# Expert additions as a TensorE loop, a ring of eight row buffers instead of ten, and query products every nine gathers

## The reference, cut to what matters

```python
def peer_mixer(h, w_q, keys_1, keys_2, u_tab, v_tab):
    q = (hf @ w_q).reshape(t, PEER_HEADS, PEER_QUERY_DIM)           # 8 heads, 256 wide
    s1 = jnp.einsum('thd,nd->thn', q[..., :half], keys_1)           # 128 keys
    s2 = jnp.einsum('thd,nd->thn', q[..., half:], keys_2)
    v1, i1 = lax.top_k(s1, PEER_TOPK)                               # 16 of each
    v2, i2 = lax.top_k(s2, PEER_TOPK)
    sc, ci = lax.top_k(cand, PEER_TOPK)                             # 16 of 256 sums
    experts = (e1 * PEER_N_KEYS + e2)
    gates = jax.nn.softmax(sc, axis=-1)
    def expert_block(args):                                         # 128 tokens at a time
        a = jax.nn.gelu(jnp.einsum('td,ted->te', hb, u_tab[eb]))
        w = gb * a
        return jnp.einsum('te,ted->td', w, v_tab[eb])
```

## Time and profile before

| | |
|---|---|
| median of 3 runs | 1461.5 us (1459.98 to 1465.24) |
| the profiled execution | 1459.02 us, span of the trace 1457.4 us |
| PE busy | 1295.8 us (89%) |
| DVE busy | 936.4 us (64%) |
| ACT busy | 658.5 us (45%) |
| POOL busy | 396.4 us (27%) |
| first gather issued, last gather issued | 164.3 us, 798.1 us |
| last gather landed | 819.4 us |

### The profile page before, as it was taken

The page is one execution under the profiler, slowest core; times in us unless marked ns, Lnnn a source line. Parts: engine busy times, 40 slices in busy tenths (PEclk is TensorE's granted clock), DMA queues, the critical chain, the costliest instruction groups (busy, mean ns, idle before and its releaser), DMA issues.

```text
span 1457.4 us, 21059 instructions
## 1 busy us (share of the span) xinstructions
PE 1295.8 (89%) x6856; PEld 930.2 (64%) x6856; DVE 936.4 (64%) x2259; ACT 658.5 (45%) x1809; POOL 396.4 (27%) x440
## 2 busy tenths in 40 slices
PE   6999888988888888777787888999999999999998
PEld 3888744434433343222332467899998887899897
DVE  6678787766767666766664566655556744655555
ACT  3444344443443434333433336555545448545554
POOL 4112345544444444444443142200001004100000
PEclk9999999999999999999999998999999999999999
DMA  8877799999999999999999621765556530455554
GB/s 330 339 265 282 272 420 420 421 423 420 421 422 421 420 421 421 422 421 422 421 421 422 246 74 43 255 203 181 184 187 240 193 116 2 159 161 186 186 187 145
DMA packets 81340, 422.50 MB, mean 290 GB/s; under 512 B 10144, under 2 KB 11472, under 8 KB 48368
## 3 DMA queue, kind: packets, MB, share of 16 engines
q0 software_dynamic: 47808, 307.91, 51.6%
q1 hardware_dynamic: 32128, 110.48, 22.7%
q10 hardware_dynamic: 1328, 3.15, 0.6%
HBM read 418.88 MB, written 2.62 MB: 289 GB/s over the span
## 4 chain that ended last, share of the span: by engine, by line
PE 54%; DMA 26%; DVE 11%; ACT 4%; issue 2%; POOL 1%; DVEq 0%; ACTq 0%; SPq 0%; POOLq 0%
DMA big<-in_experts,R 25%; PE pacc L1174 9%; PE pu L705 6%; PE pu L707 6%; PE pu L706 6%; PE pu L678 3%; DVE big L2477 3%; PE pacc L705 2%; PE pacc L706 2%; PE pacc L707 2%; PE pacc L763 2%; PE pacc L762 2%; PE pacc L764 2%; PE pu L688 1%; PE pu L1093 1%
## 5 line engine op out<-in xcount | busy, mean ns | idle before, releaser
L1174 PE MATMUL pacc<-big,early_l 128*128 128x512 f32 x1024 | 481.1, 612 | 106.8 <-ACT early_l L1508 106.8
L1174 PEld LDWEIGHTS pacc<-big,early_l 128*128 128x128 f32 x1024 | 187.3, 193 | 382.7 <-issue 380.2
L2477 DVE CUSTOM_DVE_ANT_0 big<-big,early_h 128x1024 f32<-128x1024 f32 x256 | 310.7, 1225 | 185.9 <-DMA big<-in_experts,R 184.7
L581 POOL DMA_INDIRECT big<-in_experts,R x256 | 289.5, 1131 | 363.6 <-PE pacc L1174 329.4
L463 DVE TENSOR_TENSOR ring_lo<-ring,ring_hi 128x512 fp32r<-128x512 f32 x336 | 220.0, 696 | 193.8 <-ACT ring_hi L456 193.6
L456 ACT ACTIVATE ring_hi<-ring 128x512 fp32r<-128x512 f32 x336 | 192.4, 620 | 135.2 <-PE pu L707 53.1
L1508 ACT ACTIVATE R<-R 128x1 f32<-128x1 f32 x256 | 51.4, 201 | 296.5 <-DVE R L2477 296.3
L705 PE MATMUL pu<-X2h,ring_hi 128*128 128x256 f32 x512 | 146.3, 286 | 3.2 <-DVE big L2592 3.2
L707 PE MATMUL pu<-X2h,ring_lo 128*128 128x256 f32 x512 | 145.5, 284 | 0.0
L706 PE MATMUL pu<-X2l,ring_hi 128*128 128x256 f32 x512 | 145.4, 284 | 0.0
L705 PEld LDWEIGHTS pu<-X2h,ring_hi 128*128 128x128 f32 x512 | 98.8, 193 | 4.3 <-DVE big L2592 3.6
(11 more groups left out here) (433 smaller groups left out, 2101.1 us busy)
## 6 DMA issues: line engine op xcount, KB each, us to landing
ring<-in_weights SPq DMA_DIRECT2D x208, 512.0 KB, 3.5
big<-in_ada POOLq DMA_DIRECT2D x40, 512.0 KB, 6.4
big<-in_w POOLq DMA_DIRECT2D x12, 512.0 KB, 7.4
big<-in_experts,R POOLq DMA_INDIRECT x256, 19.3
big<-in_late_q POOLq DMA_DIRECT2D x6, 512.0 KB, 8.9
bias_row<-big ACTq DMA_DIRECT2D x1, 1536.0 KB, 19.9
XT<-in_xT ACTq DMA_DIRECT2D x1, 1024.0 KB, 8.2
scr<-in_ada POOLq DMA_DIRECT2D x2, 512.0 KB, 12.2
```

Of the source, the lines that this page charges most:

```text
L581: pool.indirect_dma_start(out=pair_rows[:, m % PAIR_SLOTS, :], out_offset=None, in_=experts_d, in_offset=bass.IndirectOffsetOnAxis(ap=expe ...
L1174: last = mm(paccf[:, tt * D + half * 512:tt * D + (half + 1) * 512], diagonal[:, m % 16, :], pair_rows[:, m % PAIR_SLOTS, D + half * 512:D ...
L2477: v.tensor_tensor_reduce(out=pair_rows[:, m % PAIR_SLOTS, 0:D], in0=pair_rows[:, m % PAIR_SLOTS, 0:D], in1=h2_rows[:, u % TT, :], scale=1. ...
```

## The change

Four things change. The ring of row buffers has eight entries. Queries 4 to 15 come every nine gathers, at m = 9, 18, ... 108. Row additions 112 to 239 run as a loop of four rounds with a body of 32 additions (two units); in it the waits for the landing and for the diagonal count with the round's register. The accumulation of the first token tile's sums is closed by four small products with zeros after the loop, instead of by the `stop` flag of row addition 239, so ACT waits for one row addition more before it reads them. POOL's wait for `ada_used` at m = 8 goes, since from m = 8 on a gather waits for a row addition.

```diff
-PAIR_SLOTS = 10
+PAIR_SLOTS = 8
-QUERY_STEP = 12
+QUERY_STEP = 9
+LOOP_FIRST, LOOP_STEP = 112, 2 * TOPK
...
                 if m >= PAIR_SLOTS:
                     pool.wait_ge(s["rows_added"], m - PAIR_SLOTS + 1)
-                elif m in (4, 5, 8):
-                    pool.wait_ge(s["ada_used"], MOD_EARLY + {4: 5, 5: 7, 8: 8}[m])
+                elif m in (4, 5):
+                    pool.wait_ge(s["ada_used"], MOD_EARLY + {4: 5, 5: 7}[m])
...
-            pe.wait_ge(s["peer_copied"], EARLY_QUERIES + 2)
-            for m in range(PAIRS):
-                if query_at(m) is not None:
-                    query(query_at(m))
-                pe.wait_ge(*pair_landed(m))
-                pe.wait_ge(s["diagonals"], m + 1)
+            def add_rows(m, g=None):
+
+                sem, landed = pair_landed(m)
+                pe.wait_ge(sem, tick(g, 16 * LOOP_STEP // PAIR_SLOTS, landed))
+                pe.wait_ge(s["diagonals"], tick(g, LOOP_STEP, m + 1))
                 tt = m // TOPK % TT
                 for half in range(2):
                     last = mm(paccf[:, tt * D + half * 512:tt * D + (half + 1) * 512], diagonal[:, m % 16, :],
                               pair_rows[:, m % PAIR_SLOTS, D + half * 512:D + (half + 1) * 512],
-                              start=(m in (0, TOPK)), stop=(m in (PAIRS - TOPK - 1, PAIRS - 1)), skip_group_check=True)
+                              start=(m in (0, TOPK)), stop=(m == PAIRS - 1), skip_group_check=True)
                 last.then_inc(s["rows_added"], 1)
+
+            pe.wait_ge(s["peer_copied"], EARLY_QUERIES + 2)
+            for m in range(LOOP_FIRST):
+                if query_at(m) is not None:
+                    query(query_at(m))
+                add_rows(m)
                 if m >= 2 and query_at(m - 2) is not None:
                     key_scores(query_at(m - 2))
+            with pe.Fori(0, (PAIRS - TOPK - LOOP_FIRST) // LOOP_STEP) as g:
+                for m in range(LOOP_FIRST, LOOP_FIRST + LOOP_STEP):
+                    add_rows(m, g)
+            for b in range(4):
+                mm(paccf[:, b * T:(b + 1) * T], zeros[:, 0:P], zeros[:, :], start=False, stop=True, skip_group_check=True)
+            for m in range(PAIRS - TOPK, PAIRS):
+                add_rows(m)
                 if m == TURN:
                     turn_back(0)
             turn_back(1)
...
                 if m == TURN - 2:
-                    act.wait_ge(s["rows_added"], PAIRS - TOPK)
+                    act.wait_ge(s["rows_added"], PAIRS - TOPK + 1)
```

## The result

The changed kernel takes 1466.99 us (median of 8 runs, 1465.47 to 1467.94), the kernel before 1461.15 us beside it (8 runs, 1459.21 to 1465.24). The ratio of their times is 1.0037, with a 95% interval of 1.0028 to 1.0047. That is 5.4 us more, between 4.1 and 6.9 (the two medians alone are 5.8 us apart). 1465 was forecast, 3.2 us more than before, with a range of 1459 to 1475.

What follows compares the result with a forecast made beforehand. The prediction took the PEER layer to be bound by 256 gathers passing the DMA engines. It added 2.7 (ring at the start) + 0.3 + 0.2 (closer queries) = 3.2 us to 1461.5, giving 1464.7, stated as 1465, range 1459 to 1475.

Steps and rivals of the forecast that it cites:

- What bounds the kernel: PEER layer: 256 gathers at 2.49 us each through the DMA engines; time in which these run dry is lost one for one.
- The ring at the start: Eight buffers let the DMA engines run dry before gathers 11 to 13: +2.7 us; a slip of 1 to 7 us had chance 0.56.
- L: Time from issue to landing of an unqueued gather: taken as 5.4 us, bounded by 2.49 and 7.7 us.
- The ring in the steady part: Later gathers with eight buffers: 14.7 us from issue to landing leaves 7 to 9 us of room, cost 0.
- Closer queries: Queries every nine gathers: query 4 delays gather 17 by 0.3 us, query 5 adds 0.2, then 0 up to m = 108.
- rival 1: PE becomes the bound between gathers 20 and 110: 10 us lost, about 1472 us, slower; chance 0.22.
- The loop: Row additions 112 to 239 in rounds of 32: branches and register waits hidden under the DMA queue, cost 0.
- The prediction's own sign of being wrong: DMA engines also dry after 230 us, or at a turn of the loop, or dry nowhere.
- 2, no slip: At the start the queue never runs dry, or the first gathers return sooner: no change, 1461.5 us; chance 0.15.
- 3, code fetch at a turn: Turning back the loop fetches code at ten us a turn, three turns cost 3 to 9 us: about 1471 us; chance 0.03.
- 4, faster behind the gathers: Something in the later layers, such as PE's clock, comes out faster: below 1454 us; chance 0.04.
- the sum for L = 7.7 us: With an unqueued gather at 7.7 us: 5.0 + 0.3 + 0.2 = 5.5 us later at the last landing.

Runs made afterwards that it cites:

- six open: Kernel before, ten buffers, with POOL allowed only six unfinished gathers from gather 64 on: 1464.18 us, ratio 1.0024.
- late queries: Changed kernel with queries 4 to 15 at m = 20, 31, ... 141 and its loop from 144: 1466.47 us, ratio 1.0042 to the kernel before.
- the ring alone: Kernel before with eight row buffers in place of ten, queries still every twelve gathers, all row additions unrolled: 1465.70 us, ratio 1.0026.
- the kernel with three open: Kernel before, ten buffers, with POOL allowed only three unfinished gathers from gather 160 on: 1575.47 us in one run.
- Eight late: Kernel before, ten buffers, with at most eight unfinished gathers from gather 64 on: 1461.11 us, ratio 1.0001.
- the kernel with the later gates: Changed kernel with unit 1's exponential on ACT at m = 7 in place of 3, DVE's part at 10 in place of 5: 1465.16 us, ratio 1.0035.
- the last one: Changed kernel with unit 1's gates later, query 3 at m = 6, unit 2's searches later, queries 4 to 15 at 20, 31, ... 141: 1463.84 us, ratio 1.0023.
- Two pairs of kernels: Eight buffers and queries every nine, unrolled 1.0041, with loop 1.0037; eight buffers and queries every twelve, unrolled 1.0026, with loop 1.0028.

## Why the prediction was right, and where it was not

**What bounds the kernel: right.** In the changed kernel, dry time of the DMA engines came out in the landings nearly one for one (6.2 to 6.6 us of it against 6.5). As a rule "lost one for one" is too strong: the kernels with six open and with late queries lack about 10 and 8 us of bytes by 798 us, and have +5.6 and +4.4 us at the landings. Why is open.

**The ring at the start, 2.7 us (3.0 with query 4): right in mechanism and place, too small.** In the changed kernel 3.6 us are lost there, with the ring alone 4.1, and 3.8 [2.2, 5.3] in time. Counted from the first landing, gathers 11 to 14 landed 1.2, 1.8, 3.1 and 4.2 us later than before, where 0.3, 1.6, 2.7 and 2.4 were forecast. The term that was off is L, taken as one number. I took 5.4 us, and these four took 6.4, 5.6, 5.8 and 7.7 us from issue to landing. The last of them, issued 1.7 us behind gather 13, sets the slip, and it was costed at 2.4. The 5.4 was also luckier than its source: the transfer of the earlier trace rows did not run by itself, since 0.34 MB of weights moved beside it between 1266 and 1269 us. The other thing the forecast left out is that gathers before number 11 aren't free either: the stretch from 190 to 200 us, ahead of most of them, already lacks 1.1 us.

The Trainium skill's figure (DMA: Bandwidth & Descriptors, Anatomy of one DMA) made L an estimated 4.4 us, which the prediction set beside its own. The trace of the kernel with three open disagrees with it for these gathers: none landed in under 5.4 us.

**The ring in the steady part, 0: right in time.** Eight late cost 0.01% [-0.08, 0.10]; the one trace has 1.5 us.

**Closer queries, 0.3 + 0.2, then 0 up to m = 108: the step that failed.** The 0 was measured at 2.6 to 3.0 us. I put the chance of more at rival 1 and reckoned with averages, 21.0 us of PE work in 22.4. That average holds; PE is busy 161.25 of 182 us, where 165 was reckoned. What happens is two stalls. The step of nine puts some query work on the gathers with m % 16 = 13, where ACT takes the exponentials of the gates: the key scores of the query at 27 come at m = 29, and query 8 stands at m = 45. ACT in the changed kernel, in order of time, and then PE from 262 to 322 us:

```profile
261.55 0.38 ACT L1521 ACTIVATE big<-pm 128x256 f32<-128x256 f32 x1 [3.80 <-PE pm L1123]
261.95 1.28 ACT L1521 ACT_TABLE_LOAD   x1
...
263.67 1.28 ACT L1521 ACT_TABLE_LOAD   x1
```

```profile
265.89 12.12 PE L1174 MATMUL pacc<-big,early_l 128*128 128x512 f32 x24 [4.38 <-ACT early_l L1521]
...
302.12 1.88 PE L1174 MATMUL pacc<-big,early_l 128*128 128x512 f32 x4
306.72 5.32 PE L1174 MATMUL pacc<-big,early_l 128*128 128x512 f32 x8 [2.72 <-ACT early_l L1521]
```

ACT waits for the key scores, copies them, and then needs two table loads of 1.28 us around the exponential before it can make the next diagonal (`early_l` in the rows). PE waits 4.38 us for it. At gather 45 ACT waits for the product of the query instead, and PE waits 2.72 us. Then comes a second cost. The granted clock is 0.83 in the windows 260 to 270 and 300 to 310, which means that PE's clock stood at 1.2 in place of 2.4 GHz for 3.4 us of each, from the end of these waits on. The six additions from 265.89 take 12.12 us, where six at 1.74 take 10.4. The backlog reaches POOL some buffers later, and the DMA engines run dry from 270 and from 310 us on. The clock fell at about 266 us in all four traces that have the step of nine.

That the coincidence on ACT makes the waits is shown by the runs that move the queries. With queries at m = 20, 31, ... 141 the coincidences lie at gather 77 (scores) and 141 (query), and in both kernels with that schedule PE waits 4.38 us at the first and 2.72 at the second. All six kernels that have the coincidences have exactly these two waits; in those with the old step no PE wait between 190 and 560 us is over 2.5 us. Moving the exponentials away from those gathers was not tried.

How the cost splits between the wait and the clock is less certain. Behind the wait of 4.38 us the clock fell in all six. Behind that of 2.72 us it fell in four. The kernel with the later gates is one of the two where it did not:

```profile
300.00:310.00 10.00, 7.28 (x26) 4.49 (x25) 5.14 (x10) 5.02 (x12) 2.27 (x3) 1.00 1.02 424
...
309.05 3.67 PE L1174 MATMUL pacc<-big,early_l 128*128 128x512 f32 x8 [2.72 <-ACT early_l L1521]
```

Its two additions take 3.67 us in place of 5.32, and it lost 0.9 us from 262 to 444 us in place of 2.6, with the same two waits. That is one trace, and its gates lie elsewhere too. The room counts as well: the wait of 4.38 us at gather 77, with the clock down, left the DMA engines at 422 GB/s in the kernel with late queries and at 409 in the last one (380 to 400 us). The size of the step in the changed kernel is 2.6 to 3.0 us in the trace and 1.3 or 2.2 us in time, where the intervals overlap.

**The loop, 0: right.** Two pairs of kernels and the unbroken 422 GB/s of the page around the turns agree.

**The rivals.** 1, PE the bound between gathers 20 and 110: not as put, since there is no loss at each query, but in its place and through PE's backlog it gave about 3 of its 10 us. The prediction's own sign of being wrong, dry DMA engines after 230 us, did appear. 2, no slip: refuted. 3, code fetch at a turn: refuted for this loop, since the gap isn't there and q8 has a single packet; its ten us a turn stood on no row, and no run shows such a price. Where the prediction says that the trace disagrees with the Trainium skill (Runtime: NRT & Kernel Launch, Instruction fetch mechanics), it goes too far: the rows show no fetch at loop bodies of 410 recorded PE instructions before and 298 here, and nothing shows whether the start of the body lay outside the window that the page speaks of. 4, faster behind the gathers: refuted, the later part was not shorter.

**The sum.** 3.2 us were forecast and 5.4 [4.1, 6.9] measured. By the trace it is 3.6 us at the start and 2.6 to 3.0 from the two stalls, against 6.5 us from the first landing to the last, or 5.5 at the last landing alone. That the sum for L = 7.7 us was 5.5 too is chance: it put all of it at the start, where 3.6 us lie. The 1465 came within 2 us of the 1466.99, and the range held, though a second loss of the same order had been put at nothing.

## What to carry to other kernels

When transfers bound a stretch, cost a shallower ring where the consumers are latest and not by the steady part: here two buffers cost 0.01% from gather 64 on and 0.26% before it, and the time from issue to landing in a short window at the start against that in the middle shows it beforehand. For the room that a ring must leave, take the spread of landings (5.4 to 6.8 us unqueued, 7.7 for one issued close behind another), not the least, and the longest time from landing to issue, not its average. When work is moved to a new period, lay its places over every other period of the same queues (here 9 against 16): the averages stayed below the bound, and two coincidences made the loss.

## What the runs showed of the hardware that was not expected

Gathers of 1.05 MB that were issued with none outstanding differ by a quarter in time to landing (5.4 to 6.8 us), and six open ones, 14.9 us of transfers, don't keep the DMA engines full (413 against 421 GB/s). PE, busy for 89% of the time, dropped to the lower clock for 3.4 us behind a wait of 4.38 us, and again behind one of 2.72 us, in a stretch where its mean clock is 0.98; behind the same wait of 2.72 us it stayed at the upper clock in two of six kernels. A PE loop with a body of 32 row additions turned back without a gap on the gathers, with branches of 76 to 231 ns.
